# Three quarters of the second feed-forward product by seven products, in a decoder block of a Trainium2 kernel

## The reference

```
u = rmsnorm(h, norm_mix);  z = u @ w_in                  # 2048 x 6448
h = h + concat(rwkv7_mixer(z_rw), fox_mixer(z_fox)) @ w_out
u = rmsnorm(h, norm_mlp)
h = h + square(relu(u @ w_ff1)) @ w_ff2                  # 2048 x 8192 and 8192 x 2048
gate = sigmoid(rmsnorm(h, norm_ple) @ w_ple_gate)
h = h + gate * (p @ w_ple_proj)
out = rmsnorm(h, norm_final)
```

## Time and profile before

| what | us |
|---|---|
| median of 3 runs | 2658.65 (2653.88 to 2660.2) |
| the profiled execution, its own time | 2650.66 |
| its span, first to last instruction | 2649.1 |
| TensorE busy | 2559.5 |
| VectorE busy | 1505.6 |
| ScalarE busy | 1276.4 |
| GpSimd busy | 537.5 |

### The profile page before, as it was taken

The page is one execution under the profiler, slowest core; times in us unless marked ns, Lnnn a source line. Parts: engine busy times, 40 slices in busy tenths (PEclk is TensorE's granted clock), DMA queues, the critical chain, the costliest instruction groups (busy, mean ns, idle before and its releaser), DMA issues.

```text
span 2649.1 us, 49020 instructions
## 1 busy us (share of the span) xinstructions
PE 2559.5 (97%) x18322; PEld 2108.9 (80%) x18322; DVE 1505.6 (57%) x2008; ACT 1276.4 (48%) x1721; POOL 537.5 (20%) x381
## 2 busy tenths in 40 slices
PE   7999999999778999999999999999999999999998
PEld 5777777777577778788888888878888888888887
DVE  5556766665735565777777777743334443444443
ACT  4444444443546435688888888822222222333333
POOL 0000000000223104644545455400000000111100
PEclk9999999999889999999999999999999999999999
DMA  7555545555443333444444444564444444333333
GB/s 201 148 156 151 142 143 161 165 149 163 134 148 105 118 96 120 138 131 135 135 138 126 140 135 136 156 209 123 121 119 119 119 121 123 96 95 103 98 97 107
DMA packets 503741, 352.26 MB, mean 133 GB/s; under 512 B 57173, under 2 KB 468807, under 8 KB 502663
## 3 DMA queue, kind: packets, MB, share of 16 engines
q1 hardware_dynamic: 448567, 286.12, 37.3%
q0 software_dynamic: 10320, 35.23, 3.8%
q10 hardware_dynamic: 44800, 30.18, 3.4%
HBM read 294.21 MB, written 57.28 MB: 133 GB/s over the span
## 4 chain that ended last, share of the span: by engine, by line
PE 59%; issue 27%; DVE 5%; ACT 3%; POOL 1%; DMA 1%; SPq 1%; ACTq 0%; DVEq 0%; POOLq 0%
PE bank L1244 14%; PE acc L733 8%; PE acc L735 7%; PE acc L734 7%; PE bank L1245 7%; PE acc L1140 2%; PE acc L1141 2%; PE acc L1142 2%; ACT w_hi L1341 1%; PE bank L921 1%; POOL sumsq L2624 1%; PE acc L931 1%; PE bank L931 1%; PE bank L941 1%; PE bank L950 1%
## 5 line engine op out<-in xcount | busy, mean ns | idle before, releaser
L1903 DVE TENSOR_TENSOR w_lo<-w_raw,w_hi 128x1024 fp32r<-128x1024 f32 x292 | 359.5, 1231 | 684.0 <-ACT w_hi L1341 682.2
L1341 ACT ACTIVATE w_hi<-w_raw 128x1024 fp32r<-128x1024 f32 x292 | 308.9, 1058 | 789.7 <-PE acc L735 734.4
L1244 PE MATMUL bank<-mix,w_hi 128*128 128x512 f32 x1568 | 557.8, 393 | 4.9 <-DVE tile_sums L2427 2.1
L1245 PE MATMUL bank<-mix,w_lo 128*128 128x256 f32 x1568 | 440.4, 281 | 0.0
L733 PE MATMUL acc<-hidden,w_hi 128*128 128x512 f32 x1024 | 399.2, 390 | 6.6 <-DVE w_lo L1903 6.6
L734 PE MATMUL acc<-hidden,w_hi 128*128 128x512 f32 x1024 | 399.1, 390 | 0.0
L735 PE MATMUL acc<-hidden,w_lo 128*128 128x512 f32 x1024 | 398.9, 390 | 0.0
L1244 PEld LDWEIGHTS bank<-mix,w_hi 128*128 128x128 f32 x1568 | 294.8, 188 | 71.7 <-DVE w_lo L2393 5.7
L733 PE MATMUL acc<-a_all,w_hi 128*128 128x512 f32 x800 | 321.1, 401 | 2.1 <-DVE w_lo L1903 2.1
L735 PE MATMUL acc<-a_all,w_lo 128*128 128x512 f32 x800 | 312.8, 391 | 0.0
L734 PE MATMUL acc<-a_all,w_hi 128*128 128x512 f32 x800 | 312.3, 390 | 0.0
(11 more groups left out here) (370 smaller groups left out, 4131.7 us busy)
## 6 DMA issues: line engine op xcount, KB each, us to landing
w_raw<-in_w_ff SPq DMA_DIRECT2D x128, 512.0 KB, 3.9
w_raw<-in_w_in SPq DMA_DIRECT2D x100, 512.0 KB, 3.8
parts<-in_w_ff SPq DMA_DIRECT2D x32, 1024.0 KB, 5.8
parts<-in_w_ff SPq DMA_DIRECT2D x64, 512.0 KB, 4.9
w_raw<-in_w_out SPq DMA_DIRECT2D x32, 512.0 KB, 4.0
hid_d<-sq ACTq DMA_DIRECT2D x32, 512.0 KB, 2.6
w_raw<-in_w_ple_gate SPq DMA_DIRECT2D x32, 512.0 KB, 4.0
z_d<-ev POOLq DMA_DIRECT2D x50, 256.0 KB, 3.4
```

Of the source, the lines that this page charges most:

```text
L1244: mm(dst[:, :], wh[:, j, :], mixed(x, j), start=fresh and j == 0, stop=False, skip_group_check=True)
L1245: last = mm(dst[:, 0:HT], wl[:, j, :], mixed(x, j)[:, 0:HT], start=False, stop=j == NJ, skip_group_check=True)
L1341: A(w_hi[:, s, :, :], w_raw[:, s ^ raw_turned[0], :, :], ACT.Copy).then_inc(sg("w_hi_ready"), 1)
L1903: V.tensor_tensor(w_lo[:, s, :, 0:width], w_raw[:, s ^ raw_turned[0], :, 0:width], w_hi[:, s, :, 0:width].bitcast(F32), ALU.subtract).then ...
```

## The change

Three of the four quarters of the second matrix now go by seven products too; the last quarter goes the plain way as before, and adds its tiles to what the seven products left.

- `RING` is 24 steps. The 48 input blocks are 24 pairs, and of these 8 are resident at a time, in the eight slots of `mix` and `mix_last` that held the first matrix's activations. Step t multiplies the pairs t to t+7 (modulo 24) for output pair t modulo 8. After each step one slot gets the next pair.
- In the first 24 pairs of the first matrix GpSimd makes S1 to S4 of the hidden activations (`sum_hidden`, four subtractions and additions over 256 columns) and ScalarE's queue stores them (`hid_sums_d`). A11, A12 and A22 are read from `hid_d`.
- **Fill.** When each product of the last pair of the first matrix is done, its block is loaded for all 8 slots at once (`fill`, 1024 KB each, seven of them), split by ScalarE (`fill_hi`, 1792 and 256 columns) and by VectorE (five) or GpSimd (two) (`fill_lo`).
- **Refill.** During a step the slot's seven blocks come in four batches (`refill`: two, two, two and one block of 256 columns, issued by SP when the step's product 2, 4, 6 and 7 is done), are rounded by ScalarE (`refill_hi`) and split by GpSimd (`refill_lo`); TensorE waits for them before products 1, 3, 5 and 7 of the next step.
- **Rows.** The sums of a step (`ev`, two tiles of 512 columns) no longer go to `h`. VectorE puts them in a row pair (`sumsq`, `tmp`): a copy in the first 8 steps, and an addition to the pair loaded from `grown_d` after that (`grow_rows`). SP stores the pair (`store_rows`) and from step 8 on loads the next one (`load_rows`).
- SP loads each weight part in two transfers, since the ring's slots begin at another pair in each step.
- In the last quarter VectorE has one operation more for each tile: the tile plus the stored rows, times `rstd`, plus `h2`. GpSimd's queue loads `h2` and the rows in two pieces each.
- At the start of the first matrix VectorE and ScalarE do the last input pair's A11 earlier, and S and A22 of the pair before it later.

The core of the diff:

```diff
+    RING = 3 * PAIRS // 4
+    STEPS = PAIRS + RING
...
+            def load_second_parts(t, which):
+                p, m = PAIRS + t, t % UK
+                sums_made, turn = ((3, 1), (4, 5), (3, 5))[which]
+                sp.wait_ge(sg("weight_sums_made"), past("weight_sums_made") + 4 * (p - 1) + sums_made)
+                sp.wait_ge(sg("w_split"), FIRST + UNITS * (p - 1) + turn + 3)
+                for to, k0, n in ((m, t, UK - m), (0, (t + UK - m) % RING, m)) if m else ((0, t, UK // 2), (UK // 2, t + UK // 2, UK // 2)):
+                    if which == 0:
+                        sp.dma_start(parts[:, 0, to:to + n, :], ff2_parts[:, 0, k0:k0 + n, 2 * P * m:2 * P * (m + 1)]).then_inc(sg("part_landed0"), 16)
+                    else:
+                        sp.dma_start(parts[:, 1, to:to + n, (which - 1) * P:which * P],
+                                     ff2_parts[:, 1, k0:k0 + n, 2 * P * m + (which - 1) * P:2 * P * m + which * P]).then_inc(sg(f"part_landed{which}"), 16)
...
+            def fill(n):
+                u = FILL_TURN[n]
+                sp.wait_ge(sg("unit_done"), FIRST + 2 + UNITS * (PAIRS - 1) + n + 1)
+                if n >= 4:
+                    sp.wait_ge(sg(f"refill_landed{n % 4}"), past(f"refill_landed{n % 4}") + 32)
+                sp.dma_start(ring_parts(u, slice(HT, T))[0].bitcast(F32), hidden_block(u, slice(0, NJ))).then_inc(sg(f"refill_landed{n % 4}"), 16)
+                sp.dma_start(mix_last[:, u:u + 1, HT:T].bitcast(F32), hidden_block(u, slice(NJ, UK))).then_inc(sg(f"refill_landed{n % 4}"), 16)
...
+            def refill(t, b):
+                u, n = BATCHES[b]
+                k = (t + UK) % RING
+                if t == 0:
+                    sp.wait_ge(sg(f"refill_landed{b}"), past(f"refill_landed{b}") + FILLED[b])
+                sp.wait_ge(sg("unit_done"), FIRST + 2 + UNITS * (PAIRS + t) + (2, 4, 6, 7)[b])
+                src = (hid_d[k, :, :, 0:HT], hid_sums_d[k, :, 0:2, :], hid_sums_d[k, :, 2:4, :], hid_d[k, :, 1:2, HT:T])[b]
+                sp.dma_start(ring(u, n, t % UK, slice(HT, T)).bitcast(F32), src).then_inc(sg(f"refill_landed{b}"), 16)
...
+            def load_rows(t):
+                sp.wait_ge(sg("rows_moved"), moved(t))
+                for b in range(2):
+                    sp.dma_start(row_pair_of[b][:, :], grown_d[2 * (t % UK) + b]).then_inc(sg("rows_moved"), 16)
...
+            def store_rows(t):
+                sp.wait_ge(sg("rows_grown"), past("rows_grown") + 2 * (t + 1))
+                sp.wait_ge(sg("rows_moved"), moved(t) + (32 if t >= UK else 0))
+                for b in range(2):
+                    sp.dma_start(grown_d[2 * (t % UK) + b], row_pair_of[b][:, :]).then_inc(sg("rows_moved"), 16)
...
+            sp.wait_ge(sg("hidden_stored"), past("hidden_stored") + 16 * UK)
+            sp.wait_ge(sg("sums_stored"), past("sums_stored") + 16 * UK)
+            load_second_parts(0, 0)
+            fill(0)
+            load_second_parts(0, 2)
+            load_second_parts(0, 1)
+            fill(1)
+            fill(2)
+            fill(3)
+            fill(4)
+            load_second_parts(1, 0)
+            fill(5)
+            fill(6)
+            load_second_parts(1, 2)
+            load_second_parts(1, 1)
+            for t in range(RING):
+                if t < RING - 1:
+                    if t == 0:
+                        sp.wait_ge(sg("hidden_stored"), past("hidden_stored") + 16 * RING)
+                        sp.wait_ge(sg("sums_stored"), past("sums_stored") + 16 * RING)
+                    if t:
+                        load_second_parts(t + 1, 0)
+                    refill(t, 0)
+                    if t:
+                        load_second_parts(t + 1, 2)
+                        load_second_parts(t + 1, 1)
+                if t:
+                    store_rows(t - 1)
+                if t < RING - 1:
+                    refill(t, 1)
+                if t >= UK:
+                    load_rows(t)
+                if t < RING - 1:
+                    refill(t, 2)
+                    refill(t, 3)
...
+                    if p == PAIRS:
+                        if u in FILLS_OF_POOL:
+                            pe.wait_ge(sg("refilled"), past("refilled") + FILLS_OF_POOL.index(u) + 1)
+                        else:
+                            pe.wait_ge(sg("filled"), past("filled") + (1, 2, 3, 0, 4, 0, 5)[u])
+                    elif p > PAIRS and u % 2 == 0:
+                        pe.wait_ge(sg("refilled"), i * 4 + (past("refilled") + len(FILLS_OF_POOL) + 4 * (p - PAIRS - 1) + u // 2 + 1))
...
+            seven_products(0, PAIRS)
+            with pe.Fori(0, RING - 1) as i:
+                seven_products(i, PAIRS + 1)
...
+            def second_his(i, t):
+                p = PAIRS + t
+                product_hi(i, p, 3)
+                product_hi(i, p, 0)
+                refill_hi(i, t - 1, 1)
+                product_hi(i, p, 1)
+                product_hi(i, p, 2)
+                refill_hi(i, t - 1, 2)
+                product_hi(i, p, 4)
+                refill_hi(i, t - 1, 3)
                 for u in range(5, UNITS):
-                    product_hi(i, 2, u)
+                    product_hi(i, p, u)
+                if t < RING - 1:
+                    refill_hi(i, t, 0)
...
                 take_fifth(i, p, 3)
+            grow_tile(0, NJ, 0)
             product_lo(0, 0, 0)
-            mix_los(0, NJ - 1, "S")
+            mix_los(0, NJ, "A11")
             mix_los(0, NJ - 1, "A22")
-            grow_tile(0, NJ, 0)
-            mix_los(0, NJ, "A11")
             grow_tile(0, NJ, 1)
             product_lo(0, 0, 1)
+            mix_los(0, NJ - 1, "S")
...
+            def grow_rows(i, t):
+                dve.wait_ge(sg("hidden_summed"), i + (past("hidden_summed") + PAIRS + t + 1))
+                if t < UK:
+                    dve.wait_ge(sg("rows_moved"), i * 32 + (past("rows_moved") + 32 * t))
+                else:
+                    dve.wait_ge(sg("rows_moved"), i * 64 + (past("rows_moved") + 64 * t - 32 * UK + 32))
+                for b in range(2):
+                    if t < UK:
+                        V.tensor_copy(row_pair_of[b][:, :], ev[:, b, :]).then_inc(sg("rows_grown"), 1)
+                    else:
+                        V.tensor_tensor(row_pair_of[b][:, :], row_pair_of[b][:, :], ev[:, b, :], ALU.add).then_inc(sg("rows_grown"), 1)
...
+            def second_pair(i, t):
+                p = PAIRS + t
+                product_lo(i, p, 3)
+                take_167(i, p - 1, 4)
+                sum_22(i, p - 1)
+                product_lo(i, p, 0)
+                sum_12(i, p - 1)
+                product_lo(i, p, 1)
+                sum_21(i, p - 1)
+                product_lo(i, p, 2)
+                grow_rows(i, t - 1)
+                take_first(i, p)
+                product_lo(i, p, 4)
+                sum_11(i, p)
+                product_lo(i, p, 5)
+                take_16(i, p, 3, 2)
+                product_lo(i, p, 6)
+                take_fifth(i, p, 3)
...
+                    f = 2 * i + (f0 + b)
+                    for rows in ("h2", "grown"):
+                        dve.wait_ge(sg(f"{rows}_landed{n}"), past(f"{rows}_landed{n}") + 16)
+                    part = grown_part[:, b:b + 1, :]
+                    V.tensor_tensor(part, rows_y[:, bass.ds(f, 1), :], acc[b][:, :].rearrange("p (a t) -> p a t", a=1), ALU.add).then_inc(sg("acc_taken"), 1)
+                    dve.wait_ge(sg("acc_taken"), 2 * i + (M_FF2 + f0 + b + 3))
+                    V.tensor_tensor(part, part, rstd[:, None, :], ALU.mult).then_inc(sg("rows_grown"), 1)
...
+            with pool.Fori(0, RING) as i:
+                sum_weights(i, 2, 1)
+                sum_hidden(i, 0)
+                for which in (2, 3, 4):
                     sum_weights(i, 2, which)
...
+            def refill_lo(i, t, b):
+                u, n = BATCHES[b]
+                pool.wait_ge(sg("refill_hi_ready"), i * 4 + (past("refill_hi_ready") + UNITS + 4 * t + b + 1))
+                hi, lo = (ring(u, n, t % UK, c, None if t % UK == NJ else i) for c in (slice(0, HT), slice(HT, T)))
+                G.tensor_tensor(lo, lo.bitcast(F32), hi.bitcast(F32), ALU.subtract).then_inc(sg("refilled"), 1)
...
+            def second_sums(i, t):
+                if t > 1:
+                    refill_lo(i, t - 2, 2)
+                    refill_lo(i, t - 2, 3)
+                else:
+                    fill_lo(3)
+                sum_weights(i, PAIRS + t, 1)
+                if t == 1:
+                    fill_lo(5)
+                refill_lo(i, t - 1, 0)
+                sum_weights(i, PAIRS + t, 2)
+                sum_weights(i, PAIRS + t, 3)
+                refill_lo(i, t - 1, 1)
+                sum_weights(i, PAIRS + t, 4)
...
+            pool.wait_ge(sg("unit_done"), FIRST + 2 + UNITS * STEPS)
+            pool.wait_ge(sg("w_landed1"), 16 * (M_FF2 + 1 - SKIPPED + 3))
```

(59 more changed lines are left out.)

285 lines of the change are left out of this document (177 added, 108 removed).

## The result

| | us |
|---|---|
| changed kernel, median of 5 runs | 2667.33 (2665.69 to 2670.87) |
| kernel before, median of 5 runs | 2655.06 (2652.37 to 2660.2) |
| ratio | 1.0046, 95% interval 1.0027 to 1.0064 |

The account below looks back on a forecast made before the run. TensorE, busy 97% of the span, bounds the kernel. Second matrix: 466.1 + 173.8 + 22 + 11 + 4 = 676.9 us for 704.7; with -3 and +0.7, -30 in all, median 2629 us, range 2603 to 2667.

Parts of the forecast that it names:

- Out of the ring: Last quarter of the second matrix: weights beside a load of `h2` again, half of the old 8 us kept, 4 us.
- The steps: Ring steps: VectorE's two operations ahead of `take_first` make TensorE wait, 11 us in all, bounds 0 and 30.
- The pairs of the first matrix: `sum_hidden` fits GpSimd's gap of 5.66 us, so costs nothing; 12 us if it spilled over in 24 pairs.
- Into the ring: Fill between last pair and first step: ScalarE's surplus 11, late transfers 9, clock 2; 22 us, bounds 11 and 35.
- ScalarE's surplus and late landings: Fill: ScalarE has 11 us too much rounding work; the last block is split 9 us late; the two are added.
- a step without waits: Second matrix: each of 24 steps takes 19.42 us, a pair's time, if nothing waits; 466.1 us in all.
- the start's reorder: Start of the first matrix: the reorder removes half of waits and low clock, -3 us, bounds 0 and -5.9.
- one more operation a tile: Last quarter: VectorE's added operation is hidden under 10.9 us of matmuls; only the last tile's shows, 0.7 us.
- all hidden: Rival, chance 0.15: additions fall into GpSimd's rests, fill costs 12 us and the end 2; -53, 2606 us.
- The transfers' rival: Chance 0.16: at 209 GB/s for 135 landings slip and lengthen steps by 1.6 us each, 37 for 11; 2655 us.
- the slower rival: Chance 0.17: `take_first` waits bring the low clock back each step, 3.8 us a step, 84 for 11; 2702 us.

Follow-up runs that it names:

- experiment 1: Changed kernel with the last quarter's second-tile weights issued ahead of the rows' store: last quarter 189.4 us for 200.6, ratio to the kernel before 1.0026.
- experiment 7: On top of experiment 1, `h2` and the rows loaded in four pieces, not two: last quarter 181.7 us.
- experiment 3: Changed kernel with VectorE growing the rows behind `take_first`: steps 10 to 24 took 301.3 us for 310.5, ratio to the kernel before 1.0023.
- experiment 8: On top of experiment 3, ScalarE rounds the second refill behind the second product's weights: 19.41 us in 14 of steps 10 to 24.
- experiment 9: Changed kernel with all edits of order together, start of the first matrix kept as changed: 2628.65 us for 2652.47 of the kernel before, ratio 0.9906.
- experiment 12: As experiment 9, with the first matrix's start in the old order: 2627.84 us for 2654.91 of the kernel before, ratio 0.9916.

## Why the prediction was wrong

**The step that failed** is *Out of the ring*: "Of the 8 us I keep half: 4 us, bounds 0 and 10". It measured 26.8, half of the whole miss of 45 us. I carried the old stall over, halved it, and didn't walk SP's queue past the new items in it. The weights of the second tile had been moved behind a store whose producer stands last on VectorE (11.2 us, experiment 1), and the rows doubled the bytes of `h2`, 8 MB for 4, of which 6 come in one go (7.7 us, experiment 7). 7.9 us are left, and for the waits at the first and the third tile in them I have no cause that a run shows.

*The steps*, 11 forecast, 21.4 measured: the mechanism was right and the size off. The waits for `take_first` stood where I put them, 12.4 us as counted and 16.8 with what stands beside them. The shared port takes 0.7 us from the first addition, and from a split of the refill, not from a weight sum. What I had not in the sum is the cadence: I took 19.42 for the one pace of a pair, and it is one of two. It is 2.5 us in steps 10 to 24, and with some short stops it makes the 2.3 of steps 3 to 9. That the place of the additions was the cause is shown by experiment 3; with experiment 8 the 15 steps fall by 17.8 us, of which 2.5 are the cadence. By the Trainium skill's rule of the shared port each addition could have waited for a whole weight sum, 4.2 us a step; 0.83 was measured.

*The pairs of the first matrix*, 0 forecast, 6.9 measured. I asked only whether `sum_hidden` fits on GpSimd, and it does. ScalarE's second issue, which I didn't cost, delays the sixth split of weights by 0.5 us, and with it the read of the third product. The stops are short, 14 of 0.2 us or less, 3 us in all; the other 4 us are cadence.

*Into the ring*, 22 forecast, 27.8 measured, nearly the right number for partly wrong reasons, which is luck. 4 us were GpSimd's splits blocking VectorE's, and 8 the first refill, an item that moved past me in two queues. 16 us are left in the first step with everything mended. I had put them down to ScalarE's surplus and late landings, and no run separates these. The trace gives most of the first wait another cause: in experiment 9 too the first two splits take 4.22 and 2.57 us beside GpSimd's weight sums, where 2.01 and 0.42 come next, and TensorE waits 4.58 us for the weights split behind them. No run moves these sums away.

*Right:* a step without waits can take 19.41 us (experiment 8; in experiment 12 it takes 19.79); the start's reorder, -2.5 for -3; one more operation a tile is hidden. *The rivals:* all hidden was reached only with the edits of experiment 8, and only in the steps. The transfers' rival was wrong by amount in the steps (209 GB/s cost nothing) and right by order: what was late there was late in SP's queue. The kernel did get slower, but the slower rival didn't happen as written. Its waits came, up to 1.5 us in each of 15 steps, but the clock stayed at 1.00 through all of them; it fell only beside longer ones, to 0.82 over the first two steps and 0.95 in the quarter, and not beside each: behind the 2.95 us at 2281.93 it was 1.00. The Trainium skill ("TensorE: Matmul & The Clock Gate", section "HAM oscillation — how this bites in real kernels") tells of a loop whose wait for a transfer brings the low clock back in every turn; the waits of these 15 steps didn't.

## What to carry to other kernels

When a stage is moved behind another, write out each queue across the seam, item by item, with what each item waits for and which engine's program makes that: most of the causes here were an item standing behind one that it doesn't need, and most of these were mended by moving a line or two. A stage that saves work on the busiest engine pays with its two seams; cost these from their own queues, not from the stall of the stage that was there before. And after a wait is removed, look at once for the next one in the same loop: in experiments 1, 3 and 8 it was there, smaller.

## What the chip did that I had not expected

TensorE runs the same seven products at one of two cadences (paces), 2.77 or 2.83 us a product, at granted clock 1.00 and without a gap. In the traces here it changes between them almost only at a wait, however short, and keeps what it took: 29 pairs at 19.42 in one execution of the kernel before and at 19.79 in another. That is 11 us in the first matrix alone, 0.4% of the kernel, as much as the effect that was measured. In the changed kernel each small stop may change it. What sets it I don't know: it is no matter of the hidden sums (both cadences are there before the change and in pairs without them), nor of the program. A single profile of each kernel can so be off by 11 us and more on either side. The medians rest on several executions each, and these should hold both; which of them ran at which pace no trace shows.
